# Block 2's first projection tiles on raw turned residual, both norms as one row at the reads; column sums inside the feed-forward loop; last tiles by two banks

## What is computed

```python
u = jnp.square(jax.nn.relu(jnp.einsum('bsd,df->bsf', h, w_ff1[l])))
x = x + jnp.einsum('bsf,fd->bsd', u, w_ff2[l])
return rms_norm(x, norm_final)                 # end of block 1
...
mod = jnp.einsum('bd,de->be', silu_c, w_ada[l]) + b_ada[l]
shift1, scale1, gate1, shift2, scale2, gate2 = jnp.split(mod, 6, axis=-1)
h = modulate(rms_norm_2(x, norm1_w[l]), shift1, scale1)   # block 2
proj = jnp.einsum('btd,de->bte', h, w_in[l])
q, k, v, r, a_lr, su, sv, g_a, g_b = jnp.split(proj, IN_SPLITS, axis=-1)
```

## Time and profile before

| what | value |
|---|---|
| median of 3 runs | 1415.91 us (1415.56 to 1416.72) |
| the profiled execution, its own time | 1417.08 us |
| its span | 1415.3 us |
| mean granted TensorE clock | 0.988 of full |
| TensorE busy | 1371.8 us, 97% of the span |
| GpSimd, VectorE, ScalarE busy | 1055.6, 757.9 and 710.4 us |
| DMA | 263.02 MB, mean 186 GB/s |

### The profile page before, as it was taken

One profiled execution on the slowest core, in us unless ns is written; L12 is line 12 of the kernel. 1 busy time (PEld: TensorE's weight loads), 2 busy tenths in 40 slices (PEclk: granted clock), 3 DMA queues, 4 the chain that ended last, 5 costly groups with the idle time before them and its releaser, 6 DMA issues.

```text
span 1415.3 us, 28961 instructions
## 1 busy us (share of the span) xinstructions
PE 1371.8 (97%) x9764; PEld 1220.6 (86%) x9764; DVE 757.9 (54%) x1617; ACT 710.4 (50%) x1133; POOL 1055.6 (75%) x469
## 2 busy tenths in 40 slices
PE   7998999999999998999999999999999999999997
PEld 7887899998877876999999999999977777878885
DVE  4655433335258526249991276666588788511113
ACT  6354555555355444435556533433455555556663
POOL 6654688886777985768888877777777777788885
PEclk9999999998999999999999999999999999999999
DMA  8453677763645456545555544444445444465552
GB/s 306 153 179 120 237 282 275 284 256 134 208 144 175 159 185 250 191 132 187 180 183 186 179 164 157 154 162 155 156 159 166 164 163 163 168 248 193 193 193 89
DMA packets 72651, 263.02 MB, mean 186 GB/s; under 512 B 8208, under 2 KB 9104, under 8 KB 72224
## 3 DMA queue, kind: packets, MB, share of 16 engines
q1 hardware_dynamic: 72608, 262.46, 53.9%
HBM read 259.81 MB, written 2.62 MB: 185 GB/s over the span
## 4 chain that ended last, share of the span: by engine, by line
PE 88%; DVE 6%; issue 2%; ACT 1%; DMA 1%; POOL 1%; SPq 0%; ACTq 0%; POOLq 0%; DVEq 0%
PE bank L865 14%; PE bank L883 14%; PE bank L866 14%; PE bank L867 14%; PE bank L884 13%; PE bank L885 13%; PE bank L1271 3%; DVE arena L1741 1%; POOL wlo L433 1%; DMA raw<-stream 1%; PE bank L983 1%; PE bank L1253 1%; DMA col<-cols 0%; PE bank L941 0%; DVE bank L1369 0%
## 5 line engine op out<-in xcount | busy, mean ns | idle before, releaser
L433 POOL TENSOR_TENSOR wlo<-raw,whi 128x1024 fp32r<-128x1024 f32 x432 | 1041.6, 2423 | 320.1 <-ACT whi L503 316.9
L503 ACT ACTIVATE whi<-raw 128x1024 fp32r<-128x1024 f32 x432 | 455.8, 1057 | 347.4 <-PE bank L885 256.9
L865 PE MATMUL bank<-xh,whi 128*128 128x256 f32 x1600 | 462.4, 289 | 4.2 <-DVE xl L1332 2.4
L866 PE MATMUL bank<-xl,whi 128*128 128x256 f32 x1600 | 455.4, 285 | 0.0
L867 PE MATMUL bank<-xh,wlo 128*128 128x256 f32 x1600 | 455.0, 284 | 0.0
L883 PE MATMUL bank<-whi,xh 128*128 128x512 f32 x800 | 321.6, 402 | 12.0 <-DVE xl L1939 4.1
L865 PEld LDWEIGHTS bank<-xh,whi 128*128 128x128 f32 x1600 | 309.8, 194 | 9.4 <-POOL wlo L433 3.7
L884 PE MATMUL bank<-wlo,xh 128*128 128x512 f32 x800 | 313.1, 391 | 0.0
L885 PE MATMUL bank<-whi,xl 128*128 128x512 f32 x800 | 312.9, 391 | 0.0
L866 PEld LDWEIGHTS bank<-xl,whi 128*128 128x128 f32 x1600 | 309.9, 194 | 1.2
L867 PEld LDWEIGHTS bank<-xh,wlo 128*128 128x128 f32 x1600 | 309.6, 193 | 0.0
(11 more groups left out here) (285 smaller groups left out, 1160.3 us busy)
## 6 DMA issues: line engine op xcount, KB each, us to landing
raw<-stream SPq DMA_DIRECT2D x432, 512.0 KB, 3.3
arena<-ada SPq DMA_DIRECT2D x48, 512.0 KB, 4.8
arena<-rows SPq DMA_DIRECT2D x5, 512.0 KB, 8.6
xs<-x SPq DMA_DIRECT2D x2, 512.0 KB, 6.0
arena<-rows SPq DMA_DIRECT2D x1, 1024.0 KB, 5.5
x_spill<-xs SPq DMA_DIRECT2D x1, 1024.0 KB, 6.1
xs<-x_spill SPq DMA_DIRECT2D x1, 1024.0 KB, 6.1
out<-arena SPq DMA_DIRECT2D x2, 512.0 KB, 2.6
```

Source lines behind the costliest of these rows:

```text
L433: nc.gpsimd.tensor_tensor(wlo[:, slot, :], raw[:, slot, :], whi[:, slot, :].bitcast(F32), ALU.subtract).then_inc(lo_done, 1)
L503: nc.scalar.activation(whi[:, slot, :], raw[:, slot, :], ACT.Copy).then_inc(hi_done, 1)
L865: nc.tensor.matmul(dst, h_, xh[:, k, :], start=(k == 0), stop=False)
L866: nc.tensor.matmul(dst, h_, xl[:, k, :], start=False, stop=False)
```

## The change

In words, in the order of the run:

- The column sums of the groups 3 to 7 are taken after the twelfth turn of the feed-forward loop; DVE forms the modulation and the gains at the thirty-first of 32 units. A further gain `gain_fin` is the product of the modulated gain and `norm_final`.
- DVE writes the four residual halves one behind the other. TensorE turns the residual itself, not the normed one, into banks 4 to 7; ACT and DVE split it with `gain_fin` as scale. Two more columns of `xh` and `xl` hold the shift, so that an f tile streams 258 columns and its column 256 is the shift's part of the result.
- Both norms are one root of `ss*/D + (ss_fin * EPS/D + EPS*EPS)`. The weighted residual goes to `xn` for its squares. The root is turned into a row (`root_row`) into bank 3 and copied to `in2_r`; each q/k tile is multiplied by it at its read (`normed`), the shift's part added. The f tiles use banks 0, 1, 2, 0, 1, 2, 0, 3.
- Rows 8 and 9 (both into bank 3) stand before tile 4 and before tile 6; tile 7 waits for `gate1_done` 2.
- For the m tiles the turned residual is multiplied by gain and root (`rowed`, DVE) and shifted (`shifted`, ACT), and split again after tile 7 (`upper_normed`, `turned_normed`). The decay projection moves in front of the seventh m tile of `m_sv`. SP loads four more tiles ahead of the constants.
- The last four expert tiles are taken by banks (0, 1) and then (2, 3).

```diff
     if last == "in2_T":
-        return "xg_out", bank + 1
+        return "qk_out", (7, 6, 6, 8)[bank]
...
-        xh = sb("xh", [P, KC, T], F32R)
-        xl = sb("xl", [P, KC, T], F32R)
+        xhs = sb("xhs", [P, KC, T + 2], F32R)
+        xls = sb("xls", [P, KC, T + 2], F32R)
+        xh, xl = xhs[:, :, 0:T], xls[:, :, 0:T]
...
-            for tt in range(TT):
-                root(S("squares"), squared("fin", tt + 1), s_(SS["fin"])[:, tt:tt + 1], rs("fin", tt), 1.0 / D)
-                root(S("fin_sq"), tt + 1, rs("n1", tt), rs("n1", tt), 1.0 / D)
-            pool.wait_ge(S("unturned"), scaled_at("in2", 2))
+            pool.wait_ge(S("both_sq"), 1)
+            nc.gpsimd.tensor_tensor(rs("n1"), rs("n1"), neghalf[:, 0:2], ALU.pow).then_inc(S("roots"), 1)
+            root(S("squares"), squared("fin"), s_(SS["fin"]), rs("fin"), 1.0 / D)
...
+            upper_of(T_IN2_F + R - 1, T_IN2_F + R)
+            act.wait_ge(S("gain_set"), 1)
+            upper_raw("in2_T", gain_fin, mod[:, 0:8])
             for tt in range(TT):
                 act.wait_ge(S("x2_done"), 2 * tt + 2)
                 sums(xres[:, tt, :], tt, D, over_xg, s_(SS["fin"]), S("squares"))
...
+            upper_of(T_IN2_F + R, T_IN2_F + R + 1)
+            for b in range(4):
+                act.wait_ge(S("x2_weighted"), b + 1)
+                nc.scalar.activation(over_z[:, b * 512:(b + 1) * 512], xn[:, b // 2, (b % 2) * 512:(b % 2 + 1) * 512],
+                                     ACT.Square, accum_out=in2_sq[:, b:b + 1]).then_inc(S("in2_sq"), 1)
...
+            upper_of(T_IN2_F + R + 1, T_IN2_M + 1)
+            shifted(0, "in2_T", mod[:, 0:8])
+            upper_of(T_IN2_M + 1, T_IN2_M + R - 1)
+            act.wait_ge(S("in2_half"), 1)
+            upper_normed("in2_T", (0, 1))
+            act.wait_ge(tile_used, T_IN2_M)
+            upper_normed("in2_T", (2, 3))
...
+            LATE = 12
...
+                for first, end in ((0, LATE), (LATE, (count - 2) // 2)):
+                    with pe.Fori(first, end) as j:
...
+                    if end == LATE:
+                        late()
...
-            pairs(T_FFN, N_FFN, "ffn", "ffn", "mlp")
-            for g in range(3, 8):
-                ada_columns(g)
+            def late_columns():
+                for g in range(3, 8):
+                    ada_columns(g)
+
+            pairs(T_FFN, N_FFN, "ffn", "ffn", "mlp", late_columns)
+            pe.wait_ge(S("mod_done"), 1)
+            turn_of("in2_T", xres, "x2_done", 0, (0, 1))
+            turn_of("in2_T", xres, "x2_done", 1, (0, 1))
+            turn_of("in2_T", xres, "x2_done", 0, (2, 3))
+            turn_of("in2_T", xres, "x2_done", 1, (2, 3))
+
+            def qk2_tile(n, turned=None, half=None):
+
+                pe.wait_ge(S("x2_done" if n < 3 else "qk_out"), n + 1 if n < 3 else n - 2)
+                f_tile((T_IN2_F + n) % R, T_IN2_F + n + 1, bank[IN2_BANK[n]][:, 0:T + 2], turned, xhs, xls, half)
+
+            for n in range(3):
+                qk2_tile(n, None if n else "in2")
+            pe.wait_ge(S("roots"), rooted("in2"))
+            pe.wait_ge(S("x2_done"), 4)
+            root_row("n1", bank[3], "in2_row")
+            qk2_tile(3)
+            pe.wait_ge(S("in2_row_out"), 1)
             ada_row(8)
-            transposes("in2_T", "in2", xn)
-            pe.wait_ge(S("mod_done"), 1)
+            qk2_tile(4)
+            qk2_tile(5)
+            pe.wait_ge(S("gate1_done"), 1)
             ada_row(9)
+            qk2_tile(6)
             pe.wait_ge(S("gate1_done"), 2)
+            qk2_tile(7, half="in2_half")
+            def decays(k):
+                if k != KC - 2:
+                    return
...
-            m_group(T_IN2_M, "m_sv")
+            m_group(T_IN2_M, "m_sv", "in2n", before=decays)
...
-            for b in range(4):
+            for banks in ((0, 1), (2, 3)):
                 for c in range(N_PEER - R, N_PEER):
-                    expert_m(c, None, final=(c == N_PEER - 1), banks=(b,), used=b == 3)
+                    expert_m(c, None, final=(c == N_PEER - 1), banks=banks, used=banks == (2, 3))
...
+            def normed(n, d_, src, row, scale, done):
+
+                if n >= 2:
+                    v.wait_ge(S(done), n - 1)
+                wshift = wshifts[:, n % 2:n % 2 + 1]
+                own(nc.vector.tensor_copy(wshift, src[:, T:T + 1]))
+                own(ttt(d_, src[:, 0:T], row, ALU.mult)); own.sync()
+                if scale is None:
+                    tsc(d_, d_, wshift, None, ALU.add).then_inc(S(done), 1)
+                else:
+                    tsc(d_, d_, wshift, scale, ALU.add, ALU.mult).then_inc(S(done), 1)
...
+            for b in range(4):
+                filled("ffn", b, T_IN2_F)
+                stt(x_half(b), bank[b][:, :], rs("mlp", b // 2), x_half(b), ALU.mult, ALU.add).then_inc(S("x2_done"), 1)
...
+            shift_lower(SHIFTS["in2"], mod[:, 0:8])
+            weighted(0)
+            turned_raw("in2", gain_fin, (0, 1))
+            weighted(1)
+            turned_raw("in2", gain_fin, (2, 3))
+            weighted(2)
+            weighted(3)
...
+            for n in range(N_IN2_F):
                 v.wait_ge(tile_used, T_IN2_F + n + 1)
+                normed(n, qk[:, n, :], bank[IN2_BANK[n]], in2_r, 128 ** -0.5 if n < 4 else None, "qk_out")
+                if 2 <= n < 6:
+                    rowed("in2_T", gain_fin, in2_r, n - 2)
+                if n == 5:
+                    v.wait_ge(S("roots"), rooted("fin"))
+                    for tt in range(TT):
+                        stt(xres[:, tt, :], xres[:, tt, :], rs("fin", tt), tmp, ALU.mult, ALU.mult)\
+                            .then_inc(S("fin_done"), 1)
+                if n in (4, 6):
+                    gate_row(8 + (n - 4) // 2, gate1, "gate1_b").then_inc(S("gate1_done"), 1)
+            turned_normed("in2_T", "in2n")
```

More of the change, by code:

```diff
@@ L259, in build @@
         gain = take(16)
+        gain_fin = take(8)
         top[0] = shared
@@ L856, in _, with f_tile @@
         def _(pe):
-            def f_tile(slot, count, dst, turned=None):
+            def f_tile(slot, count, dst, turned=None, xh=xh, xl=xl, half=None):
                 pe.wait_ge(lo_done, count)
@@ L867, in f_tile @@
                     last = nc.tensor.matmul(dst, l_, xh[:, k, :], start=False, stop=(k == KC - 1))
+                    if half and k == KC // 2 - 1:
+                        last.then_inc(S(half), 1)
                 last.then_inc(tile_used, 1)
@@ L1175, in _ @@
-            for n in range(2, N_IN2_F):
-                pe.wait_ge(S("qk_out"), n - 1)
-                f_tile((T_IN2_F + n) % R, T_IN2_F + n + 1, bank[4 + n % 2][:, 0:T])
-            pe.wait_ge(S("gate1_done"), 2)
-            pe.wait_ge(S("xg_out"), 4)
-            pe.wait_ge(S("consts2_in"), 96)
-            for k in range(KC):
-                last = nc.tensor.matmul(bank[6][0:16, 0:T], wal[:, k, :], xg[:, k, :], start=(k == 0),
-                                        stop=(k == KC - 1))
```

197 lines of the change are left out of this document (121 added, 76 removed).

## The result

| | before | changed |
|---|---|---|
| median | 1416.32 us | 1429.68 us (1426.68 to 1431.96, 4 runs) |
| ratio | | 1.0093, 95% interval 1.0074 to 1.0112 |
| profiled execution, own time; span | 1417.08; 1415.3 us | 1428.11; 1426.0 us |
| E, the loop's end | 336.06 | 342.08 |
| first f tile of block 2 | E + 14.0 | E + 5.4 |

The account below looks back on a forecast made before the run. TensorE was taken as the bound, 88% of the chain, its matmul stream gapless in the feed-forward loop. +4.3 + 3.4 - 2.1 + 1.7 - 0.4 = +6.9 us gave 1422.8 us against the median 1415.91, range 1416.5 to 1427.

Parts of the forecast that it names:

- Parts 1 and 2: Feed-forward loop: 40 uncovered column matmuls, +4.3 us, then half clock over the dense matmuls behind them, +3.4 us.
- part 2: Feed-forward loop behind the column sums: half clock over dense matmuls, +3.4 us, with 0 and 5.1 kept for the range.
- The rule of the Trainium skill that the prediction weighed: Rival, chance 0.13: the clock stays full behind column sums and stalls, sum +1.8 us, 1417.7.
- Part 3: Loop's end to block 2's first m tile, decay projection included: 39.2 us against 41.3, so -2.1 us.
- Part 4: Clock in the rebuilt stage: one fall to half clock behind one of three new stalls, +1.7 us; ends none and 5.1.
- Part 5: Run's end, last expert tiles by two banks: only VectorE's idle 0.51 us before bank 1 goes, -0.4 us.
- The rival that named it: Rival, chance 0.06: xh rows 258 elements apart slow every matmul or load, 1 ns on each of 7200, 7 us more, 1430.

Follow-up runs that it names:

- e1: Kernel before with only the column sums of groups 3 to 7 moved after the loop's twelfth turn, 40 matmuls in a row; 1423.92 us, 1.0052.
- s1: Kernel before with only the column sums in the loop, spread as eight matmuls after each of turns 4, 6, 8, 10 and 12; 1419.95 us, 1.0032.
- e4: Changed kernel with shift columns made by VectorE inside the loop and the normed product kept in PSUM; 1423.2 us, 1.0046.
- a1: Changed kernel with its 40 column matmuls spread as five groups of eight over the loop; 1429.55 us, 1.0088.
- a2: Changed kernel with xl 256 and uh 512 bytes further on than in the kernel before, experts' rows 256 apart; 1421.90 us, 1.0037.
- e2: Kernel before with only the rows of xh and xl at 258 elements, the two extra columns unused; 1421.14 us, 1.0032.
- x5: Kernel before with rows of 258, experts' rows too, and gaps that put xl 256 bytes further on; 1414.85 us, 0.9992.
- x2: Kernel before, rows of 256, with 64 unused bytes between xh and xl; 1420.53 us, 1.0029.
- x3: Kernel before with rows of 258, experts' rows 256 apart, xl 256 and uh 512 bytes further on; 1409.25 us, 0.9959.

## Why the prediction was wrong

**Parts 1 and 2, right.** 7.7 forecast, 8.1 measured alone (e1), and the split between matmuls and clock by s1 is 4.4 and 3.7 for 4.3 and 3.4. In the changed kernel's own profiled execution they took 6.1, with one short low stretch of 3.4 us, the shortest of those that part 2 weighed. The rule of the Trainium skill that the prediction weighed ("TensorE: Matmul & The Clock Gate", section "HAM oscillation — how this bites in real kernels": only long gaps in which TensorE idles are harmful) would have made it 4.3. Here the clock fell behind 40 one-column matmuls that the records show as busy (0.57 and 0.58 in the windows behind them), so the measurement decides against it.

**Part 3, mis-sized by 4.6 us in this execution.** From E: first f tile 5.4 for 3.45; tiles 0 to 2 end at 15.9 for 13.0, 1.9 by the late start and the rest by the half clock at 348.6 (part 4's term); from the root row to tile 3 2.7 for 2.1; tiles 3 to 6 13.4 for 13.2; from tile 6's end to tile 7 3.5 for 2.5; the last one 1.7 for 1.95. With the decays 43.8 where 39.2 was forecast and 41.3 stood before. The first step that failed is the durations of two VectorE operations. The small shift has no duration of its own in the prediction, whose times leave it under 0.4 us; it took 2.29. `normed`'s shift-and-scale was put at 0.33, an estimate between two values and read from no row; it took 1.26, 1.97 and 1.93, and 0.35 when undisturbed, so the estimate was good for an idle GpSimd. Both operations lie wholly in SBUF, and GpSimd was at a tile. The Trainium skill, "SBUF — State Buffer", section "SBUF: two separate sides", says that VectorE and GpSimd share one pair of ports under an exclusive lock, which a VectorE operation with two SBUF inputs or in a two-port mode needs; whoever starts first has it for its whole instruction. By that rule the shift (two SBUF inputs) waits for GpSimd, and so does the shift-and-scale if it runs in such a mode, which no row shows. The traces agree: 2.29 us and 1.26 to 1.97 us beside GpSimd's tiles, and e4's 0.48 us for the one whose input is in PSUM. The prediction neither looked for this nor gave it a rival.

**Part 4, right by luck.** One fall was forecast for the stage, behind one of the three waits that are new in it (before tile 3, tile 7 and the first m tile). The changed kernel's profile has one, but behind the wait before the first f tile (3.45 us), which part 3 had at 1.4 us and part 4 did not count; the three named ones, 2.33, 3.37 and 1.57 us, are followed by none. a1's and a2's profiles have three falls. So the changed kernel's stage by itself would fit the Trainium skill's rule too; what speaks against it are the falls behind 2.35 (a1), 2.40 (a2) and 2.07 us (e4). Between the changed kernel and a1, alike in the stage, the first m tile's distance from E differs by 3.4 us.

**Part 5, right.** -0.4 forecast, -0.5 measured.

**What was missing from the sum: the layout, 5.3 us.** This is the larger step that failed. Part 3 put the two more columns at 0.2 us, "in the rounding", and nothing in the sum stands for the buffers that they move; e2, with these rows and nothing else, measured 5.3. The rival that named it had 0.06, the right sign and nearly the size (7), and the wrong cause. It reasoned with a nanosecond on each matmul that reads long rows; but the f tiles get quicker, with such rows (x5) and with `xl` moved by 64 bytes alone (x2) alike, and the loss in the experts' m tiles comes with `xl` standing 64 bytes off (x2 has it without such rows) or with weight loads out of rows of 258 (x5 against x3). Why 64 bytes matter and 256 do not, no run here tells.

Together: parts 1, 2 and 5 hold to 0.4 us, the layout is 5.3, and the stage is left with 0.5 where -2.1 + 1.7 was forecast: 8.1 + 5.3 - 0.5 + 0.5 = 13.4. Of the 6.5 us by which the forecast missed, 5.3 are the layout. How much the stage missed by is less certain, between 0.9 us by this remainder, good to some 4, and 2.9 by the profiles (+2.5 for -0.4).
